# The first FFN's gate and up products as seven block products per slab, with the activations in six parts

## The chip, the cores and the metric

The kernel runs on one NeuronCore of a Trainium2 chip, as one launch. The metric is the device time of that core in microseconds (us). The profile splits the core into TensorE (PE, with its weight loads as PEld), VectorE (DVE), ScalarE (ACT), GpSimd (POOL) and SyncE (SP), which issues the DMAs. The engines run their own instruction streams in order and meet only at semaphores.

## The reference

A two-layer transformer trunk on 512 latent and 256 context tokens, 1024 wide: layer 0 mixes with gated linear attention, layer 1 with windowed attention, and each layer ends in a SwiGLU FFN with 2816 hidden units. The change touches the FFN of layer 0, which runs on all 768 tokens:

```python
def swiglu(h, w_in, w_out):
    g, u = jnp.split(h @ w_in, 2, axis=-1)
    return (jax.nn.silu(g) * u) @ w_out

x = x + g2 * swiglu(rmsnorm(x, norm_ffn[i]) * (1.0 + sc2) + sh2, ffn_w_in[i], ffn_w_out[i])
ctx = ctx + cg2 * swiglu(rmsnorm(ctx, norm_ffn[i]) * (1.0 + csc2) + csh2, ffn_w_in[i], ffn_w_out[i])
```

The gains sc2, sh2, g2 come from another product, SiLU(c) with `w_ada` (1024 x 6144 for each layer), of which the kernel computes 256 columns at a time: a "unit". Everything is float32.

## The kernel before

**Slabs.** All weights pass through in slabs of 256 columns. A slab is loaded (1 MB where it has 1024 rows), ACT copies it to `w_hi` in TensorE's rounded float32 format (L1260), DVE subtracts to get the rest `w_lo` (L1749, over the raw slab), and TensorE adds up three products for each pair of blocks: `w_hi x_hi`, `w_hi x_lo`, `w_lo x_hi` (L609). There are two slab buffers, and two sets of three PSUM banks. SP loads slab n once slab n-2 is done (`slab_done`), TensorE starts slab n when its `w_lo` is there (`wlo_ok`) and its banks are free (`out_free`).

**The first FFN** (`ffn(0, F0)`) has 34 slabs. 22 are gate/up slabs: 128 gate and 128 up columns, 8 k-chunks, all 768 tokens, first the 512 latent ones, then the 256 of the context. That is 48 matmuls of 512 columns and 48 of 256. After such a slab ACT applies SiLU to the gate (L1547), DVE multiplies by the up part (L2228), ACT rounds (L1550) and DVE subtracts (L2234), which gives one 128-row chunk of activations `a_hi`, `a_lo`. The chunks come in three parts of 8, 8 and 6 (`PARTS`), since the buffer holds 8. After each part come four down slabs, which multiply the part by 256 columns of `w_out`, and DVE adds the result to `xT` (`residual`, L1863, four instructions). A down slab has as many k-chunks as the part has chunks.

**Units.** 28 of these 34 slabs also carry a unit: SP loads 1 MB of `w_ada` into the one buffer `ada_w`, after the unit before has been used (`ada_done`); DVE multiplies and adds it up over 16 instructions (`unit_acc`, L1848 and L1852), TensorE sums over partitions (`unit_sum`, four small matmuls, in the trace eight records with their halves), and DVE stores the result (`store_sum`, L1830 to L1837).

**Order on DVE.** In a gate/up slab: `unit_acc` of the slab, the split of the next slab, `store_sum`, the multiply, the subtract. In a down slab: `unit_acc`, the split of the next, `store_sum`, the residual. DVE and ACT run in the order written; nothing schedules them.

**The head.** Before the FFN, DVE and ACT make `h_hi` and `h_lo` chunk by chunk (`normal`, L1803 and L1812; `modulate`, L1310), while TensorE already works on the raw rows of the first slab.

Of the kernel before, what the change touches and what calls it, by code (L numbers as in the profile page):

```python
# [24 lines left out]
F32 = mybir.dt.float32  # L25
# [7 lines left out]
P = 128  # L33
# [20 lines left out]
KV0 = F0 + FFN_SLABS  # L54
# [13 lines left out]
def trunk(nc, x, c, ctx_in, c_ctx, w_ada, b_ada, norm_mix, norm_ffn, gla_w_in, gla_w_gate_up, gla_b_gate_up,  # L68
# [26 lines left out]
    w_hi = [at(f"w_hi{s}", W + 2 * s * SLAB, [P, DC, 256], F32R) for s in range(2)]  # L95
    w_raw = [at(f"w_raw{s}", W + (2 * s + 1) * SLAB, [P, DC, 256]) for s in range(2)]
    w_lo = [at(f"w_lo{s}", W + (2 * s + 1) * SLAB, [P, DC, 256], F32R) for s in range(2)]
# [5 lines left out]
    a_lo = at("a_lo", A + DC * ROW, [P, DC, T], F32R)  # L103
    gla_q = at("gla_q", A, [P, GH, 4, T])
# [12 lines left out]
    ssq = at("ssq", TM + 6 * ROW, [P, T])  # L117
    ada_pre.append(ada_w)
# [130 lines left out]

    gw_ok, gwh_ok, gwl_ok, gl_done, gl_ok = sem("gw_ok"), sem("gwh_ok"), sem("gwl_ok"), sem("gl_done"), sem("gl_ok")  # L250
# [139 lines left out]
    def _(sp):  # L390
        def load_slab(n, i, pieces, kc=8):
# [4 lines left out]
            elif Q0 < n < SO0:  # L396
# [3 lines left out]
                sp.wait_ge(whi_ok, n - 1)  # L400
# [206 lines left out]
    def _(pe):  # L607
# [3 lines left out]
        def slab(n, i, rhs, segs, kc=8, before={}, k_wait=None, turns=None, by_chunk=False, sums=None, between=None,  # L611
# [6 lines left out]
            pe.wait_ge(wlo_ok, n + 1 + 2 * i)  # L618
# [9 lines left out]
            for z, (chunks, sgs) in enumerate(passes):  # L628
                for k in range(kc):
# [176 lines left out]
        def first_slab(n, e, segs, turn=None):  # L806
# [6 lines left out]
            pe.wait_ge(wlo_ok, n + 1)  # L813
# [89 lines left out]
        def fill(h, k, ch):  # L903
# [3 lines left out]
            if k == 0 and ch == 0:  # L907
                pe.wait_ge(wlo_ok, n + 1)
# [1591 lines left out]
```

## Time and profile before

| what | value |
|---|---|
| time, median of 3 runs | 1621.3 us (1621.28 to 1621.32) |
| span of the profiled execution | 1618.6 us; the runs are 2.7 us above it |
| PE busy | 1582.3 us, 98% of the span |
| PEld busy | 1345.5 us, 83% |
| DVE busy | 920.9 us, 57% |
| ACT busy | 575.2 us, 36% |
| chain that ended last | PE 86%, DVE 5%, ACT 5% |
| granted TensorE clock | full, but for the first slice (0.8) |
| DMA | 156.2 MB, mean 97 GB/s |

The busy share of PE counts modelled ends that overlap, so the pace of TensorE is read from the distance between the starts of its matmuls. The chain names the work that each later piece waited for. The profiled execution's own time beside its span isn't recorded; the runs above stand for it.

### The profile page before, as it was taken

To read this page: it belongs to the slowest core of one execution; us is meant where nothing else is said; L and a number is where in the kernel's file an instruction comes from. 1 tells how busy PE (TensorE), PEld (TensorE's weight loads), DVE (VectorE), ACT (ScalarE), POOL (GpSimd) and SP (SyncE) were. 2 spreads that over 40 slices of the span, in tenths; PEclk is the share of its full clock that TensorE was granted. 3 is DMA by queue.
4 is the path that set the end of the run, shared out by engine and by line. 5 is a ranking of instruction groups with operands and counts; after the bars stand their busy time and mean duration, and the time that the engine had idled before them with its cause. 6 is when DMAs were issued, how large, how long until landed. Compare 5 with 4: busy or idle time off the path is not lost.

```text
span 1618.6 us, 23967 instructions
## 1 busy us (share of the span) xinstructions
PE 1582.3 (98%) x9424; PEld 1345.5 (83%) x9424; DVE 920.9 (57%) x1592; ACT 575.2 (36%) x829; POOL 100.3 (6%) x95
## 2 busy tenths in 40 slices
PE   7999999999999999999999999989999999999998
PEld 5789988888888888888888888877778888888886
DVE  5665536544576667556666555888856533333334
ACT  5225457542342111122102124567744431222222
POOL 0000000000000000000000000046630000000003
PEclk8999999999999999999999999999999999999999
DMA  9442300013234334433343413320002323332332
GB/s 334 117 132 71 113 27 27 27 53 105 79 105 129 119 122 123 128 119 116 130 125 109 130 59 111 109 74 1 2 27 79 104 85 97 104 99 83 104 91 91
DMA packets 197438, 156.20 MB, mean 97 GB/s; under 512 B 6754, under 2 KB 194318, under 8 KB 197358
## 3 DMA queue, kind: packets, MB, share of 16 engines
q1 hardware_dynamic: 197358, 155.10, 31.5%
q8 instruction: 54, 0.88, 0.2%
q14 instruction: 26, 0.21, 0.1%
HBM read 149.84 MB, written 2.10 MB: 94 GB/s over the span
## 4 chain that ended last, share of the span: by engine, by line
PE 86%; DVE 5%; ACT 5%; issue 1%; DMA 1%; SPq 1%; DVEq 0%; ACTq 0%
PE ps L609 84%; PE ps L1145 1%; ACT pr L1703 1%; DVE w_lo L1749 1%; DMA ada_pre<-in_w_ada 1%; DVE scaled L1803 1%; DVE h_lo L1812 1%; ACT w_hi L1260 1%; PE ps L1150 1%; SPq L407 0%; DVE row_max L2394 0%; DVE q_st L2339 0%; ACT h_hi L1310 0%; DMA w_raw<-in_ffn_w_out 0%; ACT r_act L1460 0%
## 5 line engine op out<-in xcount | busy, mean ns | idle before, releaser
L609 PE MATMUL ps<-h_hi,w_hi 128*128 128x512 f32 (+1 forms) x1392 | 499.9, 359 | 1.4 <-DVE w_lo L1749 1.4
L609 PE MATMUL ps<-h_lo,w_hi 128*128 128x512 f32 (+1 forms) x1392 | 490.6, 352 | 0.0
L609 PE MATMUL ps<-h_hi,w_lo 128*128 128x512 f32 (+1 forms) x1392 | 490.4, 352 | 0.0
L1749 DVE TENSOR_TENSOR w_lo<-w_raw,w_hi 128x2048 fp32r<-128x2048 f32 (+1 forms) x88 | 197.1, 2240 | 201.9 <-ACT w_hi L1260 201.9
L609 PEld LDWEIGHTS ps<-h_hi,w_hi 128*128 128x128 f32 x1392 | 263.7, 189 | 47.0 <-issue 10.7
L1260 ACT ACTIVATE w_hi<-w_raw 128x2048 fp32r<-128x2048 f32 (+1 forms) x88 | 165.2, 1877 | 374.4 <-DMA w_raw<-in_ffn_w_in 200.0
L609 PEld LDWEIGHTS ps<-h_hi,w_lo 128*128 128x128 f32 x1392 | 263.6, 189 | 36.3
L609 PEld LDWEIGHTS ps<-h_lo,w_hi 128*128 128x128 f32 x1392 | 264.0, 190 | 35.7
L609 PE MATMUL ps<-a_hi,w_hi 128*128 128x512 f32 (+1 forms) x528 | 187.9, 356 | 0.1
L609 PE MATMUL ps<-a_lo,w_hi 128*128 128x512 f32 (+1 forms) x528 | 186.9, 354 | 0.0
L609 PE MATMUL ps<-a_hi,w_lo 128*128 128x512 f32 (+1 forms) x528 | 186.7, 354 | 0.0
L1852 DVE SCALAR_TENSOR_TENSOR u_acc<-ada_w,c_pre,u_acc 128x256 f32<-128x256 f32 x448 | 180.0, 477 | 0.0
L597 POOL TENSOR_SCALAR pr<-pr,rden 128x384 f32<-128x384 f32 x64 | 82.6, 1298 | 819.8 <-DVE rden L2406 819.5
L1547 ACT ACTIVATE tmp<-ps 128x512 f32<-128x512 f32 (+1 forms) x63 | 30.8, 524 | 259.4 <-PE ps L609 259.4
L609 PEld LDWEIGHTS ps<-a_hi,w_hi 128*128 128x128 f32 x528 | 99.8, 189 | 15.9 <-issue 1.6
L609 PEld LDWEIGHTS ps<-a_hi,w_lo 128*128 128x128 f32 x528 | 99.8, 189 | 13.9
L609 PEld LDWEIGHTS ps<-a_lo,w_hi 128*128 128x128 f32 x528 | 99.8, 189 | 13.6
L1830 DVE TENSOR_TENSOR u_acc<-ps,every 128x128 f32<-128x128 f32 x32 | 9.4, 293 | 140.1 <-PE ps L609 140.1
L1863 DVE SCALAR_TENSOR_TENSOR xT<-ps,mods,xT 128x256 f32<-128x256 f32 (+3 forms) x94 | 56.3, 654 | 56.8 <-PE ps L609 55.2
L609 PE MATMUL ps<-go,w_hi 128*128 128x256 f32 (+1 forms) x256 | 65.0, 345 | 0.3 <-ACT r_act L1460 0.3
L2228 DVE TENSOR_TENSOR tmp<-tmp,ps 128x512 f32<-128x512 f32 (+1 forms) x63 | 35.8, 596 | 48.7 <-ACT tmp L1547 48.7
L2234 DVE TENSOR_TENSOR a_lo<-tmp,a_hi 128x768 f32 (+3 forms) x42 | 34.7, 825 | 43.1 <-ACT a_hi L1550 43.1
(264 smaller groups left out, 1986.8 us busy)
## 6 DMA issues: line engine op xcount, KB each, us to landing
w_raw<-in_ffn_w_in SPq DMA_DIRECT2D x88, 512.0 KB, 4.9
ada_w<-in_w_ada SPq DMA_DIRECT2D x41, 1024.0 KB, 5.2
w_raw<-in_ffn_w_out SPq DMA_DIRECT2D x32, 512.0 KB, 4.4
w_raw<-in_gla_w_in SPq DMA_DIRECT2D x24, 512.0 KB, 4.9
ada_pre<-in_w_ada SPq DMA_DIRECT2D x7, 1024.0 KB, 11.6
w_raw<-in_ffn_w_out SPq DMA_DIRECT2D x16, 384.0 KB, 3.6
w_raw<-in_gla_w_o SPq DMA_DIRECT2D x8, 512.0 KB, 6.8
w_raw<-in_swa_w_o SPq DMA_DIRECT2D x8, 512.0 KB, 4.7
```

What stands on the lines that cost most here:

```text
L597: pool.tensor_scalar(pr[i % 4][:, 0:384], pr[i % 4][:, 0:384], rden[:, i % 4:i % 4 + 1], None, ALU.mult)\
L609: return pe.matmul(o, w, r, start=start, stop=stop, skip_group_check=skip)
L1145: last = pe.transpose(bank(4 + r, t * P, P), pr[i % 4][:, t * P:(t + 1) * P], ident[:, :])
L1150: last = pe.transpose(bank(6, (r * (nb - 3) + t - 3) * P, P), pr[i % 4][:, t * P:(t + 1) * P], ident[:, :])
L1260: act.activation(w_hi[s][:, 0:kc, :], raw_of(n)[:, 0:kc, :], ACT.Copy).then_inc(whi_ok, 1)
L1547: last = act.activation(tmp[s][:, sg[0]:sg[1]], seg(3 * s, 0, sg), ACT.Silu)
L1703: act.activation(pr[i % 4][:, 0:nk + 1], ps[:, sb:sb + nk + 1], ACT.Exp, bias=neg_max[:, i % 4:i % 4 + 1], scale=HD ** -0.5, accum_out=den ...
L1749: dve.tensor_tensor(w_lo[s][:, 0:kc, :], raw_of(n)[:, 0:kc, :], w_hi[s][:, 0:kc, :].bitcast(F32), ALU.subtract).then_inc(wlo_ok, 1)
L1852: last = dve.scalar_tensor_tensor(acc[:, m, :], ada_w[:, k, :], c_pre[:, k, m:m + 1], acc[:, m, :], ALU.mult, ALU.add)
L1863: last = dve.scalar_tensor_tensor(xs, seg(slab_banks(n), ch, sg), mods[:, bass.ds(gate + d0 + ch, 1), int(sg == CTX)], xs, ALU.mult, ALU.add)
L2228: last = dve.tensor_tensor(tmp[2 + s][:, sg[0]:sg[1]], tmp[s][:, sg[0]:sg[1]], seg(3 * s, 1, sg), ALU.mult)
L2234: dve.tensor_tensor(lo, tmp[2 + s][:, a:T], hi.bitcast(F32), ALU.subtract).then_inc(a_ok, 1)
```

## The change

The first three gate/up slabs stay as they were. In each of the other 19, the 256 x 1024 weight block times the 1024 x 768 token block is seen as 2 x 2 times 2 x 2 blocks: gate and up rows by two halves of k, two halves of k by two halves of 384 tokens. Strassen's scheme in Winograd's form computes it with seven block products in place of eight. Each product has 4 k-chunks, three matmuls each, of 384 columns: 84 matmuls a slab.

- Weights: four sums of blocks (`form_sum`, 512 elements a partition) on DVE, seven forms rounded by ACT (`form_high`) and seven subtractions by DVE (`form_low`), in place of one copy and one subtraction of 2048 elements.
- Tokens: once, after h is made. ACT writes the full h as well (`h_full`), DVE makes four sums and four low parts, ACT four high parts, 1536 elements each.
- Results: ACT copies partial sums out of PSUM (`part_sum`, four of 384 elements), DVE adds (`gate_sum_one`, `up_sum_one`, `up_sum_two`, `gate_sum_two`), then SiLU in two halves, the multiply and the split of the activations.
- There is one buffer for each form, so a form of the next slab waits for the product that used it in this one.
- Parts of 4, 4, 4, 3, 3, 4 chunks in place of 8, 8, 6: the first FFN has 24 down slabs in place of 12, with 3 or 4 k-chunks each. The token sums need the room.
- Units stand in a table: all four down slabs of the first three parts, two of the next two, and the last one to three gate/up slabs of a part. There are 28 as before.
- The first FFN is written out, not looped.

```diff
+PARTS0 = [(0, 4), (4, 4), (8, 4), (12, 3), (15, 3), (18, 4)]
...
+        if part_ == 0 and j_ == 3 or 0 < part_ < 5 and j_ >= fc_ - 2 or part_ == 5 and j_ > 0:
+            UNIT_AT[n_ + j_] = 12 + len(UNIT_AT)
...
+        def product(n, j):
+            q, s = SEVEN[n], n % 2
+            if j == 0:
+                pe.wait_ge(out_free[s], n // 2)
+            if q == 0 and j in (1, 3, 4, 5):
+                pe.wait_ge(sl_ok, (1, 3, 4, 5).index(j) + 1)
+            if j in (3, 4, 5):
+                pe.wait_ge(sn_ok, 4 * q + j - 2)
+            if j == 6:
+                pe.wait_ge(g_ok, q + 1)
+            pe.wait_ge(fl_ok, 7 * q + j + 1)
...
+        def part_sum(n, i):
+            act.wait_ge(pd_ok, 6 * q + (1, 2, 4, 6)[i])
+            if i == 1:
+                act.wait_ge(a_ok, IN0[n] - 1)
+            act.activation(dst, bank(b0 + int(i == 1), 0, HT), ACT.Copy).then_inc(sn_ok, 1)
...
+                if after:
+                    form_sum(n + 1, 0)
+                    form_low(n + 1, 0)
+                gate_sum_one(n)
+                if last_a is not None:
+                    store_sum(last_a)
+                if after:
+                    form_sum(n + 1, 1)
+                    form_sum(n + 1, 2)
+                    form_low(n + 1, 1)
+                    form_low(n + 1, 2)
+                    up_sum_one(n)
+                    if a_ is not None:
+                        unit_acc(a_)
+                    form_low(n + 1, 3)
+                    form_sum(n + 1, 3)
+                    up_sum_two(n)
+                    form_low(n + 1, 4)
+                    form_low(n + 1, 5)
...
+                gate_sum_two(n)
+                if after:
+                    form_low(n + 1, 6)
+                times_gate(n)
+                low0(n)
...
+                if last_a is not None:
+                    store_sum(last_a)
+                if a_ is not None:
+                    unit_acc(a_)
+                if e < 3:
+                    split(n + 1, 0, fc)
+                if part < 5:
+                    residual(n, 0, BOTH, 40, 2 * e, None)
```

**DVE in a gate/up slab.** Before, the end of one slab in the loop: the split of the next (2048 elements), `store_sum`, the multiply and the subtract.

```order
L1830 TENSOR_TENSOR u_acc_131<-ps,every_133 128x128 [waits or_ok,turned]
L1833 ISA
L1834 TENSOR_REDUCE den<-u_acc_131 128x4 [waits up_ok]
L1835 REGISTER_ALU
L1837 ISA [waits up_ok]
L1837 TENSOR_TENSOR mods<-den,vec 128x4
L2226 REGISTER_ALU
L2228 TENSOR_TENSOR tmp_83<-tmp_81,ps 128x256 [waits sg_ok]
L2228 TENSOR_TENSOR tmp_83<-tmp_81,ps 128x512
L2234 ISA [waits ah_ok]
L2234 TENSOR_TENSOR a_lo<-tmp_83,a_hi 128x768
```

After, the second half of a slab without a unit. `t_lo` and `w_lo_62` are low parts of the next slab's forms, `t_sum` a sum of its blocks, `tmp` the gate and up values.

```order
L2562 TENSOR_TENSOR t_lo_107<-t_sum_102,form_hi_65 128x512 [waits fh_ok]
L2562 TENSOR_TENSOR w_lo_62<-w_raw_60,form_hi_66 128x4x128 [waits fh_ok]
L2583 TENSOR_TENSOR tmp_97<-ps,tmp_97 128x384 [waits sn_ok,pd_ok]
L2562 TENSOR_TENSOR t_lo_108<-t_sum_103,form_hi_67 128x512 [waits fh_ok]
L2557 TENSOR_TENSOR t_sum_104<-w_raw_60 128x512 [waits pd_ok]
L2588 TENSOR_TENSOR tmp_97<-tmp_95,tmp_97 128x384 [waits sn_ok]
L2562 TENSOR_TENSOR w_lo_62<-w_raw_60,form_hi_68 128x4x128 [waits fh_ok]
L2562 TENSOR_TENSOR t_lo_109<-t_sum_104,form_hi_69 128x512 [waits fh_ok]
L2593 TENSOR_TENSOR tmp_95<-ps,tmp_95 128x384 [waits slab_done]
L2562 TENSOR_TENSOR t_lo_111<-t_sum_106,form_hi_70 128x512 [waits fh_ok]
L2598 TENSOR_TENSOR tmp_97<-tmp_95,tmp_97 128x768 [waits sg_ok]
L2538 TENSOR_TENSOR a_lo<-tmp_97,a_hi 128x768 [waits ah_ok]
```

Where one split and two multiplies stood, DVE now does form work for the next slab between the sums that free this slab's banks.

**DVE in a down slab.** Before: the residual of the slab behind its wait, then the unit of the next slab.

```order
L1863 ISA [waits slab_done]
L1863 ISA
L1863 SCALAR_TENSOR_TENSOR xT<-ps,mods,xT 128x256
L1863 ISA
L1863 SCALAR_TENSOR_TENSOR xT<-ps,mods,xT 128x512
L1863 ISA x2
L1863 SCALAR_TENSOR_TENSOR xT<-ps,mods,xT 128x256
L1863 ISA
L1863 SCALAR_TENSOR_TENSOR xT<-ps,mods,xT 128x512
L1842 REGISTER_ALU
L1848 TENSOR_SCALAR u_acc_131<-ada_w,c_pre 128x256 [waits in_unit]
L1848 TENSOR_SCALAR u_acc_131<-ada_w,c_pre 128x256
```

After: the split (1024 elements) for the next slab, the residual of this one, `store_sum`, the next unit.

```order
L2005 TENSOR_TENSOR w_lo_63<-w_raw_61,out_hi_w_72 128x1024 [waits whi_ok]
L2121 SCALAR_TENSOR_TENSOR xT<-ps,mods,xT 128x256 [waits slab_done]
L2121 SCALAR_TENSOR_TENSOR xT<-ps,mods,xT 128x512
L2121 SCALAR_TENSOR_TENSOR xT<-ps,mods,xT 128x256
L2121 SCALAR_TENSOR_TENSOR xT<-ps,mods,xT 128x512
L2088 TENSOR_TENSOR u_acc_155<-ps,every_157 128x128 [waits or_ok,turned]
L2092 TENSOR_REDUCE den<-u_acc_155 128x4 [waits up_ok]
L2095 TENSOR_TENSOR mods<-den,vec 128x4 [waits up_ok]
L2106 TENSOR_SCALAR u_acc_155<-ada_w,c_pre 128x256 [waits in_unit]
```

The four kinds of work are the same, the split is half as long, and there are twice as many slabs over which they come.

**PE at the third product.** Before, a gate/up slab has waits at its first matmul only (this is the end of one and the start of a down slab).

```order
L609 MATMUL ps<-h_hi,w_hi_59 128x256
L609 MATMUL ps<-h_lo,w_hi_59 128x256
L609 MATMUL ps<-h_hi,w_lo_63 128x256
L1053 REGISTER_ALU
L1053 COMPARE_AND_BRANCH
L1068 UNCONDITIONAL_BRANCH
L1068 ISA
L625 REGISTER_ALU [waits wlo_ok]
L609 MATMUL ps<-a_hi,w_hi_58 128x512 [waits a_ok,out_free0]
L609 MATMUL ps<-a_lo,w_hi_58 128x512
```

After, between the third and the fourth product of a slab:

```order
L677 MATMUL ps<-h_hi,form_hi_66 128x384
L677 MATMUL ps<-h_lo,form_hi_66 128x384
L677 MATMUL ps<-h_hi,w_lo_62 128x384
L677 MATMUL ps<-h_sums_hi,form_hi_67 128x384 [waits fl_ok,sn_ok]
L677 MATMUL ps<-h_sums_lo,form_hi_67 128x384
L677 MATMUL ps<-h_sums_hi,t_lo_108 128x384
L677 MATMUL ps<-h_sums_hi,form_hi_67 128x384
```

The fourth product waits for its form's low part and for ACT's copy of the first partial sum (`sn_ok`).

## Rows read from the trace of the kernel before

**Rows 1.** Busy time by engine: stretch, PE, PEld, DVE, ACT, POOL, PEclk, DMA.

```profile
466.00:980.00 514.00, 513.33 (x3086) 447.09 (x3087) 329.09 (x682) 101.95 (x107) 0.00 (x0) 1.00 0.38 118
```

**Rows 2.** The chain of waits about the first FFN: start, us, what.

```profile
462.40 1.81 ACT w_hi L1260
...
464.24 2.30 DVE w_lo L1749
...
466.67 533.36 PE ps L609 x3207
```

**Rows 3.** Timeline of PE in a gate/up slab pair: start, us, matmul.

```profile
632.02 0.39 PE L609 MATMUL ps<-a_lo,w_hi 128*128 128x512 f32 x1
632.25 0.39 PE L609 MATMUL ps<-a_hi,w_lo 128*128 128x512 f32 x1
632.47 0.28 PE L609 MATMUL ps<-a_hi,w_hi 128*128 128x256 f32 x1
632.59 0.28 PE L609 MATMUL ps<-a_lo,w_hi 128*128 128x256 f32 x1
```

**Rows 4.** Timeline of PE in the attention scores: 384 columns.

```profile
1109.76 0.85 PE L609 MATMUL ps<-k_st,q_st 128*128 128x384 f32 x4
1110.45 0.28 PE L609 MATMUL ps<-m_both,ident_b 128*128 128x256 bf16 x1
```

**Rows 5.** Timeline of DVE over one gate/up slab that carries a unit.

```profile
655.29 0.29 DVE L1830 TENSOR_TENSOR u_acc<-ps,every 128x128 f32<-128x128 f32 x1 [5.61 <-PE ps L609]
...
656.09 0.16 DVE L1837 TENSOR_TENSOR mods<-den,vec 128x4 f32 x1 [0.18 <-DVE den L1834]
657.07 1.02 DVE L2228 TENSOR_TENSOR tmp<-tmp,ps 128x256 f32<-128x256 f32 x2 [0.82 <-ACT tmp L1547]
659.24 0.96 DVE L2234 TENSOR_TENSOR a_lo<-tmp,a_hi 128x768 f32 x1 [1.15 <-ACT a_hi L1550]
660.11 0.61 DVE L1848 TENSOR_SCALAR u_acc<-ada_w,c_pre 128x256 f32<-128x256 f32 x2
660.64 5.62 DVE L1852 SCALAR_TENSOR_TENSOR u_acc<-ada_w,c_pre,u_acc 128x256 f32<-128x256 f32 x14
666.18 2.28 DVE L1749 TENSOR_TENSOR w_lo<-w_raw,w_hi 128x2048 fp32r<-128x2048 f32 x1
```

**Rows 6.** Timeline of DVE in a down slab: residual, then the unit.

```profile
622.06 2.19 DVE L1863 SCALAR_TENSOR_TENSOR xT<-ps,mods,xT 128x256 f32 x4 [0.21 <-issue]
624.17 0.60 DVE L1848 TENSOR_SCALAR u_acc<-ada_w,c_pre 128x256 f32<-128x256 f32 x2
```

**Rows 7.** Groups of DVE instructions by form: busy us, mean ns, idle before.

```profile
L1852 DVE SCALAR_TENSOR_TENSOR u_acc<-ada_w,c_pre,u_acc 128x256 f32<-128x256 f32 x448 | 180.0, 477 | 0.0
...
L2228 DVE TENSOR_TENSOR tmp<-tmp,ps 128x512 f32<-128x512 f32 x42 | 28.7, 684 | 31.9 <-ACT tmp L1547 31.9
...
L2228 DVE TENSOR_TENSOR tmp<-tmp,ps 128x256 f32<-128x256 f32 x21 | 8.8, 421 | 16.8 <-ACT tmp L1547 16.8
...
L2385 DVE TENSOR_TENSOR w_lo<-w_raw,w_hi 128x512 fp32r<-128x512 f32 x8 | 5.4, 672 | 0.0
```

**Rows 8.** Groups of ACT instructions by form.

```profile
L1547 ACT ACTIVATE tmp<-ps 128x512 f32<-128x512 f32 x42 | 25.0, 595 | 65.2 <-PE ps L609 65.2
...
L1663 ACT ACTIVATE w_hi<-w_raw 128x512 fp32r<-128x512 f32 x8 | 5.1, 632 | 0.0
```

**Rows 9.** DMA issues from 600 to 800 us: count, KB, us to landing.

```profile
ada_w<-in_w_ada SPq DMA_DIRECT2D x11, 1024.0 KB, 5.2
```

**Rows 10.** Timeline of ACT while the h vectors are made.

```profile
449.58 1.36 ACT L1310 ACTIVATE h_hi<-scaled,mods 128x512 fp32r<-128x512 f32 x2 [0.84 <-DVE scaled L1803]
```

**Rows 11.** Busy time by engine early in the kernel, columns as in rows 1.

```profile
20.00:31.00 11.00, 8.61 (x83) 4.89 (x81) 6.17 (x11) 6.24 (x10) 0.00 (x0) 0.71 1.10 350
```

**Rows 12.** Timeline of PE just after that stretch.

```profile
32.11 0.63 PE L609 MATMUL ps<-h_hi,w_lo 128*128 128x512 f32 x1
32.53 0.63 PE L609 MATMUL ps<-h_hi,w_hi 128*128 128x512 f32 x1
```

More of the change, by code:

```diff
@@ L1069, in ffn @@
                     for e in range(2):
[L1070 removed]
+                        slab(n + e, i, a_in, segs, kc=fc, k_wait=ready)
                 if l == 1 and after:
@@ L1074, in ffn, with ready @@
                 n += 4
-        ffn(0, F0, BOTH, 2)
+        def product(n, j):
[9 more added lines that the diff above has]
+            pe.wait_ge(fl_ok, 7 * q + j + 1)
+            o = bank(slab_banks(n) + (0, 1, 2, 0, 1, 0, 2)[j], 0, HT)
+            low = form_from(n, j, w_lo, t_lo)
+            x_hi, x_lo = token_form(j)
+            for k in range(4):
+                for i, (w, x) in enumerate(((form_hi[j], x_hi), (form_hi[j], x_lo), (low, x_hi))):
+                    last = mm(o, w[:, k, :], x[:, k, :], start=(k == 0 and i == 0 and j in (0, 1, 2, 6)),
+                              stop=(k == 3 and i == 2), skip=True)
+            last.then_inc(pd_ok if j < 6 else slab_done, 1)
+        first_slab(F0, 0, BOTH, turn=U1 - 1)
+        slab(F0 + 1, 0, h_in, BOTH, k_wait=h_wait(1, 2), joint=True)
+        slab(F0 + 2, 0, h_in, BOTH)
+        for n in range(F0 + 3, KV0):
+            if n in SEVEN:
+                for j in range(7):
+                    product(n, j)
+                    if j == 1 and n - 1 in UNIT_AT:
+                        unit_sum(UNIT_AT[n - 1])
+            else:
+                part, e, fc = OUT0[n]
+                done = PARTS0[part][0] + fc
+                def ready(k, done=done, fc=fc):
+                    if k in (0, fc - 1):
+                        pe.wait_ge(a_ok, done - (k == 0))
+                slab(n, 0, a4_in, BOTH, kc=fc, k_wait=ready,
+                     before={(0, 1): lambda: unit_sum(UNIT_AT[n - 1])} if n - 1 in UNIT_AT else {})
         first_slab(KV0, KV_EDGE, BOTH)
@@ new lines, in _ @@
+        modulate(1, 0, BOTH, sh, 0, 2)
+        bias_row(0)
+        modulate(1, 0, BOTH, sh, 2, 6)
+        act.wait_ge(bz_ok, 1)
+        act.wait_ge(zg_ok, 1)
+        for sg in BOTH:
+            last = act.activation(tmp[0][:, sg[0]:sg[1]], tmp[0][:, sg[0]:sg[1]], ACT.Silu,
+                                  bias=bz[:, 0, int(sg == CTX):int(sg == CTX) + 1])
+        last.then_inc(sg_ok, 1)
+        modulate(1, 0, BOTH, sh, 6, 8)
+        split(n + 2)
+        act.wait_ge(zp_ok, 1)
+        act.activation(a4_hi[:, 0, :], tmp[2][:, :], ACT.Copy).then_inc(ah_ok, 1)
@@ new lines, in _ @@
+        n, sh = F0, 24
+        inverse(5)
+        normal(1, 0, BOTH, sh, 0, 1)
+        split(n + 1)
+        normal(1, 0, BOTH, sh, 1, 6)
+        dve.wait_ge(slab_done, n + 1)
+        dve.tensor_copy(bz[:, :, :], bank(7, 0, 4).rearrange("p (c m) -> p c m", m=2)).then_inc(bz_ok, 1)
+        for sg in BOTH:
+            last = dve.tensor_tensor(tmp[0][:, sg[0]:sg[1]], seg(0, 0, sg), rb[:, sg[0]:sg[1]], ALU.mult)
+        last.then_inc(zg_ok, 1)
+        for sg in BOTH:
+            last = dve.tensor_tensor(tmp[2][:, sg[0]:sg[1]], seg(0, 1, sg), rb[:, sg[0]:sg[1]], ALU.mult)
@@ new lines, in _ @@
+        last.then_inc(out_free[0], 1)
+        normal(1, 0, BOTH, sh, 6, 8)
+        split(n + 2)
+        dve.wait_ge(out_free[0], n // 2 + 1)
+        dve.wait_ge(sg_ok, 1)
+        for sg in BOTH:
+            c_ = int(sg == CTX)
+            last = dve.scalar_tensor_tensor(tmp[2][:, sg[0]:sg[1]], tmp[2][:, sg[0]:sg[1]], bz[:, 1, c_:c_ + 1],
+                                            tmp[0][:, sg[0]:sg[1]], ALU.add, ALU.mult)
+        last.then_inc(zp_ok, 1)
+        low0(n)
+        dve.wait_ge(hf_ok, DC)
```

362 lines of the change are left out of this document (316 added, 46 removed).

## The prediction

> **What bounds the kernel now.** I read the page first: TensorE is busy for 98% of the span, the chain that ended last is 86% TensorE. Then the windows over the stretch in question, from 466 us (third gate/up slab) to 980 us: TensorE is busy 513 of 514 us at the full clock, VectorE 329 us, ScalarE 102 us, DMA at 0.38 [rows 1]. Then the chain: from 466.67 us on it is one unbroken piece of TensorE [rows 2]. So removed matmul time comes back in full as long as VectorE keeps up. The reader is to see the other side too: VectorE is the second engine, at 64%, and the change gives it work and takes none of its large items away.
>
> **TensorE, what goes.** Matmuls start 0.23 us apart at 512 columns (632.02, 632.25, 632.47) and 0.12 at 256 [rows 3]. So a gate/up slab before is 48 x 0.2265 + 48 x 0.12 = 16.64 us. At 384 columns four take 0.69 us, 0.173 each [rows 4]; a slab of seven products is 84 x 0.1733 = 14.56 us. Nineteen slabs save 19 x 2.08 = 39.5 us. Down slabs keep their matmuls in sum: 8.32 us with four chunks (24 of each width), 6.24 with three. A unit's sums cost TensorE 0.56 us, as before.
>
> **VectorE, what comes.** Durations: 512 elements take 0.672 us [rows 7], but successors start 0.08 us before the end: 14 unit instructions of 0.477 fill 5.62 us, 0.40 each [rows 5, 7]. I take 0.60 for 512 elements. 384 elements from PSUM lie between 0.421 and 0.684 [rows 7]: 0.55, in a row 0.47. 768 elements: 0.96, in a row 0.87 [rows 5]. A unit: 660.11 to 666.18 = 6.07. Storing it: 655.29 to 656.25 = 0.96, with its waits 1.05. Residual: 622.06 to 624.17 = 2.11 [rows 6]. Split: 2.28 for 2048 elements [rows 5], 1.1 for 1024.
> A seven-product slab then has 11 form instructions (6.6), four sums (1.9), multiply and subtract (1.75): 10.25 us, where before split, multiply and subtract made 4.2. Two round trips over ScalarE stand in its order: 1.15 us before the subtract, as now [rows 5], and about as much before the multiply (half a SiLU, 0.46, and the last form, 0.63 by [rows 8], between `gate_sum_two` and `form_low` 6). That is 12.5 us, within 14.56. With a unit it is 18.6, 4.0 too long.
>
> At the whole of a part of four with six units VectorE has 4 x 10.25 + 4 x 1.1 + 4 x 2.11 + 6 x 7.05 = 96 us of work; TensorE has 58.2 + 33.3 + 6 x 0.56 = 94.9. Before, TensorE had 103.2 for the same and VectorE some 67. The two engines are now level, and each wait of one for the other is lost. Where the waits come:
>
> - Slab after a unit slab: its fourth product needs ScalarE's copy of the first partial sum, and that stands in ScalarE's queue behind the rounding of the late activations. TensorE waits the 4.0 us. The first down slab then waits for the last chunk: after `slab_done` come sum 0.55, SiLU 0.46, multiply 0.96, rounding 0.85, subtract 0.96 and hand-overs, 4.2 us, and that slab's last chunk comes after 4.1; with a store and unit in front of it, 1.4 us.
> - First to second down slab: 4.2, store 1.05, unit 6.07, split 1.1, hand-over 0.2: 12.7 against 8.9, so 3.8.
> - Second to third, third to fourth: `ada_w` is one buffer. The load is issued when a unit ends and lands 5.2 us later [rows 9], with 0.2 for the issue, then 6.07: 11.5 from unit to unit, against 8.9. VectorE's own work (10.4) is nearly as long. 2.6 each.
> - Fourth to next part: unit, one sum and one form in place of the split, then the residual (2.11) between forms 1 and 2: 2.9.
>
> Parts 1 and 2: 94.9 + 4.0 + 1.4 + 3.8 + 5.2 + 2.9 = 112.2 against 103.2, +9.0 each, **+18.0**. Part 0 (one new slab): -2.1 + 3.8 + 5.2 + 2.9 = **+9.8**. Parts 3 and 4 (three chunks, units in two gate/up and two down slabs): TensorE 43.7 + 25.0 + 2.2 = 70.9; waits 4.0, 1.0, then 12.4 against 6.8 (5.6), and 2.4 after the third down slab, with 0.4: 84.3 against 77.1, +7.2 each, **+14.4**. Part 5 (three unit slabs in a row, none in its down slabs): -8.3 + 4.2 + 5.0 + 1.5 = **+2.4**.
>
> **The head.** ScalarE has 0.84 us free per chunk of h [rows 10] and gets 1.05 more (`h_full`, two copies). Chunks come about 0.5 us later each, six times, and the last two add 1.4 before ScalarE reaches the copy of the third slab, which starts TensorE's unbroken run [rows 2]: 4.4 us. After it VectorE has, beside the old work, four token sums of 1.76 (1536 elements by the 2048 row) and two low parts: the first product of the first new slab is ready 18.5 us after that start, where TensorE comes after 16.6: 1.9. Two more low parts, a unit and a split then stand ahead of the first down slab, 4.8 late. **+11.2**; bounds 3 (all but the first 4.4 hidden) and 16.
>
> Sum: 18.0 + 9.8 + 14.4 + 2.4 + 11.2 = +55.8 us. The profiled execution's span is 1618.6 and the runs' median 1621.3; 2.7 lie around the span, untouched. 1621.3 + 55.8 = **1677 us**, a span of 1674.
>
> Not in the sum: six-part residuals on the last part's ScalarE and VectorE chain (squares, raw rows) fit 8.3 us with little to spare, 0 to 3 us. SP gets 24 loads more of half the size, on a queue that is idle, 0.
>
> **A rule against the trace.** The 14 unit instructions start 0.40 us apart though each lasts 0.477 [rows 5, 7], so they overlap. The Trainium skill, "VectorE: DVE Perf Modes", section "The DRAIN you can't avoid", says the next operation doesn't start before the pipe has emptied. The trace disagrees by those 0.08 us an instruction.
> As a mechanism of its own, VectorE starting each instruction only at the end of the one before, it would give 19 x 11 x 0.07 + 28 x 16 x 0.077 = 49 us more, 1726; I give it 0.01.
>
> **Rivals.**
> 1. The waits pack. VectorE works through without a hole, since the sum of its work, 96 us, is what a part takes, under 103.2. The place is the down slabs: if `ada_w` came earlier than 5.2 us and ScalarE's trips fell beside form work, parts 1 and 2 would gain 7 each, 3 and 4 6 each, part 5 8, part 0 2, less 8 for the head, 28 in all: 1593. It decides once the holes of a part stay under 7 us. Against it: both of the trips are there in the present trace, with nothing to put in between, and they alone are 2.3 us a slab.
> 2. VectorE hides all, as the diff's interleaving seems to aim at: 1621.3 - 39.5 = 1582. Against it stands the 18.6 us of a unit slab.
> 3. It costs more. The unit's load now meets the slab's, issued 1.3 us behind it; at the 16 unit loads next to down slabs up to 1.7 us more each (half a slab's share of 5.2 us), 27 us. And the clock: where TensorE stood idle for a fifth of the time the granted clock was 0.71 [rows 11], and matmuls of 512 columns started 0.42 us apart [rows 12] in place of 0.23, the lower of its levels, 1.2 GHz. There are now some 25 holes of 2.5 to 5.6 us. A block product (12 x 0.173 = 2.1 us) at half pace costs 2.1 more; behind holes in down slabs such a loss is mostly hidden by the unit, in gate/up slabs not. 0 to 25 us. Together up to 1729; I take 1707 for this case.
> The Trainium skill, "TensorE: Matmul & The Clock Gate", section "HAM oscillation — how this bites in real kernels", says that a wait repeated in each tile throttles the engine again each time; that is this rival's second half, and the present trace has too few holes in this stretch to say.
> 4. The change doesn't do what it says: half the slabs wait for token sums or forms and no order results. Nothing in the waits points to it.
>
> **Chances.** Forecast (slower, 1652 to 1695) 0.69. No overlap on VectorE 0.01. Rival 3 0.17. Rival 1 0.07, rival 2 0.02. Small waits that about cancel, within 0.2% of 1621 (what a measurement of this kernel can tell): 0.02, and a small loss up to 1652, 0.02. So faster 0.09, same 0.02, slower 0.89. The range for eight in ten, 1645 to 1708: at its low end the head costs 3 and the parts' 84 us of waits are three tenths less, at its high end half of rival 3 comes in, and 3 to 5 on the last part's chain.
>
> **What would show it.** In the profile after: PE busy in the first FFN falls by about 40 us while the stretch gets longer; VectorE over 85% busy there. Matmuls of 384 columns 0.173 apart. The down slabs with units start 11.5 us apart, the first of each part 12.7 after its start. In gate/up slabs, the hole is before the fourth product, released by a ScalarE copy from PSUM. `ada_w` lands 5.2 us after its issue, or 7 (rival 3). PEclk under 1.00 in those slices would be rival 3's other half. The prediction is wrong if units run in less than 6 us, or if VectorE shows under 75%.

## The result, and the profile after

The changed kernel takes 1681.8 us (median of four runs, 1680.6 to 1687.1) against 1621.3: a ratio of 1.038, interval 1.036 to 1.040. It is slower by 60.5 us; the forecast was 55.8, 1677. The profiled execution is the longest of the four, span 1685.4, and its +66.8 is what the lines below add up to; the spans of the other three runs were 1678.9 to 1680.7, 4.7 to 6.5 us shorter.

The page, busy time by engine, and the chain of waits:

```profile
span 1685.4 us, 23337 instructions
PE 1584.0 (94%) x9196; PEld 1363.8 (81%) x9196; DVE 1083.0 (64%) x1907; ACT 665.2 (39%) x1051; POOL 100.1 (6%) x95
PE 68%; DVE 18%; ACT 6%; DMA 4%; issue 3%; SPq 1%; DVEq 0%; ACTq 0%
```

Over the whole span VectorE is busy 64% of the time, 57% before. The stretch has to be read by itself; there it was 64% before [rows 1]. These are windows of the profile after (columns as in [rows 1]): the part of four chunks from 551 to 664 us, a part of three, and the whole to 1064, where the FFN ends; the unbroken piece of TensorE at full clock of [rows 1, 2] is gone.

```profile
551.00:664.00 113.00, 102.42 (x571) 93.54 (x572) 95.83 (x202) 34.70 (x60) 0.00 (x0) 0.92 0.37 112
777.00:862.00 85.00, 72.64 (x403) 66.25 (x402) 71.31 (x149) 25.56 (x45) 0.00 (x0) 0.92 0.35 105
466.00:1064.00 598.00, 533.68 (x2979) 482.56 (x2977) 502.62 (x1009) 190.79 (x321) 0.00 (x0) 0.93 0.35 105
```

VectorE works 95.8 us in the first of these windows, near the 96 of the forecast for a part, and 84% of the whole stretch. TensorE's waits from 466 to 1060 us, sorted by what ended them (us in total, times, longest):

```profile
PE ps L677 <- DVE w_lo L2005: 35.7, 14, 3.9
PE ps L677 <- ACT tmp L1752: 21.3, 6, 3.7
PE ps L677 <- DVE w_lo L2562: 4.6, 3, 2.4
PE ps L677 <- DVE a_lo L2538: 1.5, 2, 0.7
```

They come to 63 us. One sign that the forecast named didn't come: TensorE's busy time in the first FFN was to fall by about 40 us. It is 533.7 us (last window above) against 531.3 before (466 to 998 us), though 39.5 us of matmuls are gone: many of those that are left take longer, as the last rows of this section show.

The two large rows are the two kinds that the forecast named: the split of a down slab's weights behind a unit, and ScalarE's copy of the first partial sum. The second kind, in ScalarE's timeline at a slab after a unit slab:

```profile
606.93 0.84 ACT L1764 ACTIVATE a_hi<-tmp 128x768 fp32r<-128x768 f32 x1 [1.63 <-DVE tmp L2598]
607.68 0.85 ACT L1752 ACTIVATE tmp<-ps 128x384 f32<-128x384 f32 x2
```

The copy (L1752) is ready to go long before, but stands behind the rounding of the activations (L1764), and that waits for VectorE's multiply (L2598), late by the unit. TensorE meets it before the fourth product:

```profile
608.21 0.69 PE L677 MATMUL ps<-h_sums_hi,form_hi 128*128 128x384 f32 x1 [3.52 <-ACT tmp L1752]
```

The first kind, in the chain of waits over two down slabs (start, us, what):

```profile
635.98 5.55 DVE u_acc L2110 x14
...
641.55 5.24 DMA ada_w<-in_w_ada
...
646.81 0.62 DVE u_acc L2106 x2
647.42 4.83 DVE u_acc L2110 x13
...
652.99 5.22 DMA ada_w<-in_w_ada
```

Unit, load, unit, load: 11.44 us from one load to the next (641.55, 652.99), with nothing else in it. The load has its 5.24 us, as before [rows 9]. And TensorE, where such a hole ends, starts at half pace, 0.43 us apart at 512 columns in place of the 0.23 of [rows 3]:

```profile
631.29 0.80 PE L677 MATMUL ps<-a_hi,out_hi_w 128*128 128x512 f32 x1 [3.08 <-DVE w_lo L2005]
631.88 0.63 PE L677 MATMUL ps<-a_lo,out_hi_w 128*128 128x512 f32 x1
632.31 0.63 PE L677 MATMUL ps<-a_hi,w_lo 128*128 128x512 f32 x1
```

That is the lower of the clock's two levels, 1.2 GHz, as in [rows 12]; the granted clock is 0.92 to 0.93 over the parts, and was 1.00. Of the 18 holes of 2 us and more between 466 and 1064 us, 16 are followed by matmuls at that pace, even the shorter ones (551.77, after 2.42 us; 654.15, after 2.24); the holes of under 1 us leave next to none. This agrees with the Trainium skill, "TensorE: Matmul & The Clock Gate", section "HAM oscillation — how this bites in real kernels", that waits which come again in each tile throttle the engine again each time.

### The profile page after: what moved, and what is told of

The parts are those of the page before. It is cut to its first block, busy times and chain, and to the rows that moved or that the text cites. A ratio compares the mean times of both kernels' runs of the same rounds, so it can differ in the third digit from the quotient of the medians.

```text
span 1685.4 us, 23337 instructions
## 1 busy us (share of the span) xinstructions
PE 1584.0 (94%) x9196; PEld 1363.8 (81%) x9196; DVE 1083.0 (64%) x1907; ACT 665.2 (39%) x1051; POOL 100.1 (6%) x95
## 4 chain that ended last, share of the span: by engine, by line
PE 68%; DVE 18%; ACT 6%; DMA 4%; issue 3%; SPq 1%; DVEq 0%; ACTq 0%
PE ps L677 66%; DVE u_acc L2110 7%; DMA ada_w<-in_w_ada 2%; DVE w_lo L2005 1%; PE ps L1257 1%; DVE t_lo L2562 1%; DMA w_raw<-in_ffn_w_in 1%; ACT w_hi L1375 1%; ACT pr L1959 1%; DVE t_sum L2557 1%; DVE u_acc L2106 1%; DMA ada_pre<-in_w_ada 1%; DVE w_lo L2562 1%; DVE scaled L2061 1%; DVE tmp L2598 1%
## 5 line engine op out<-in xcount | busy, mean ns | idle before, releaser
L677 PE MATMUL ps<-h_hi,w_lo 128*128 128x512 f32 (+2 forms) x936 | 338.0, 361 | 0.0
L677 PE MATMUL ps<-h_hi,w_hi 128*128 128x512 f32 (+1 forms) x784 | 293.7, 375 | 4.2 <-DVE w_lo L2005 4.0
L677 PE MATMUL ps<-h_lo,w_hi 128*128 128x512 f32 (+1 forms) x784 | 286.4, 365 | 0.0
L677 PEld LDWEIGHTS ps<-h_hi,w_hi 128*128 128x128 f32 x784 | 148.5, 189 | 34.5 <-issue 6.2
L677 PEld LDWEIGHTS ps<-h_lo,w_hi 128*128 128x128 f32 x784 | 148.7, 190 | 24.0
L677 PE MATMUL ps<-a_hi,out_hi_w 128*128 128x512 f32 (+1 forms) x352 | 128.6, 365 | 35.2 <-DVE w_lo L2005 33.7
L677 PE MATMUL ps<-a_lo,out_hi_w 128*128 128x512 f32 (+1 forms) x352 | 124.4, 353 | 0.0
L677 PE MATMUL ps<-h_hi,form_hi 128*128 128x384 f32 x304 | 103.7, 341 | 5.0 <-DVE w_lo L2562 4.6
L677 PE MATMUL ps<-h_sums_lo,form_hi 128*128 128x384 f32 x304 | 106.7, 351 | 0.0
L677 PE MATMUL ps<-h_lo,form_hi 128*128 128x384 f32 x304 | 104.4, 343 | 0.0
L677 PE MATMUL ps<-h_sums_hi,form_hi 128*128 128x384 f32 x152 | 55.1, 363 | 21.3 <-ACT tmp L1752 21.3
## 6 DMA issues: line engine op xcount, KB each, us to landing
ada_pre<-in_w_ada SPq DMA_DIRECT2D x7, 1024.0 KB, 11.5
```

What stands on the lines that cost most here:

```text
L677: return pe.matmul(o, w, r, start=start, stop=stop, skip_group_check=skip)
```

## The experiments

Kernels of one group ran on one chip, with the kernel before beside them: 1622.0 us in the first group, 1621.6 in the second, 1621.4 in the third.

### 1. Less of a unit's work

```diff
-            for k in range(DC):
+            for k in range(1 if a >= 12 else DC):
...
+                    dve.wait_ge(mod_ok, last_a + 2)
```

`unit_acc` then has 2 instructions in place of 16. The second line makes VectorE, in a down slab, wait for its own store of the last unit.

> The changed kernel, with the 28 units of the first FFN computing one of their eight k-chunks on VectorE (2 instructions in place of 16; the other seven are left out). Loads, TensorE sums and stores stay. Theory (VectorE's unit work on top of the form work makes the holes): a unit costs 0.6 us in place of 6.1, VectorE falls to some 60% of a part, the holes of 2.5 to 4 us go and with them the half-pace stretches; left are about 1 us at each part's start of down slabs and the head's 4 us. 1590 to 1600 us. Rival A (the form work alone, or ScalarE's round trips, makes the holes): holes in gate/up slabs stay, over 1630. Rival B (twice as many down slabs cost by themselves): the holes between down slabs stay, over 1630.

Measured: 1593.0 us, ratio 0.982 (0.981 to 0.984), inside the expectation. The same shortening of the units on the kernel before (without that wait), as a control:

> The kernel before with the same units shortened in the same way (seven of eight k-chunks left out). VectorE was 64% busy there and never waited for: every theory expects 1621 us within 1.

Measured: 1621.6, ratio 0.9997 (0.9987 to 1.0007). So the units cost nothing before, and 89 us after. Without them the change does bring a gain, 29 us. A window of that run (its parts of four start at 537.94, 633.06 and 728.46 us):

```profile
551.00:664.00 113.00, 113.00 (x680) 105.89 (x679) 77.84 (x140) 43.47 (x76) 0.00 (x0) 1.00 0.43 131
```

TensorE is never idle, and VectorE works 69% of the window. The matmul arithmetic of the forecast stands: 94.9 us were worked out for TensorE in such a part, and the starts are 95.1 and 95.4 apart.

### 2. Six parts alone

The parts, the table of units and all else of the change, but ordinary slabs: no token sums, no forms.

```diff
-        if f_ + j_ >= 3:
-            SEVEN[n_ + j_] = f_ + j_ - 3
...
-                for j in range(7):
-                    product(n, j)
...
+                slab(n, 0, h_in, BOTH,
+                     before={(0, 1): lambda: unit_sum(UNIT_AT[n - 1])} if n - 1 in UNIT_AT else {})
```

> The changed kernel with ordinary gate/up slabs in place of the seven products (no forms, no token sums), but with its six parts, 24 down slabs and its table of units. Theory: the down slabs with units are bound by unit to unit, 5.2 for the load, 0.2 and 6.1, 11.5 us against TensorE's 8.9, whatever the gate/up slabs do: 12 us a part in parts 0 to 2, 8 in parts 3 and 4, so 1621 + 53 = 1674, and up to 10 more by half pace after the holes. No hole in gate/up slabs. Rival (the form work on VectorE is what costs): 1621 to 1630 us, since VectorE is back to 4.2 us a gate/up slab.

Measured: 1685.8, ratio 1.040 (1.039 to 1.042), at the top of what was expected (1674 and up to 10 more), and no faster than the whole change. TensorE does the full eight products here, and VectorE in a part of four works only 66.4 us of 113:

```profile
551.00:664.00 113.00, 106.64 (x620) 90.03 (x618) 66.42 (x145) 18.61 (x20) 0.00 (x0) 0.96 0.34 103
```

So a net loss of this size needs no form work at all. It takes short down slabs: TensorE passes one in 8.9 us and the chain of unit and load takes 11.5. The holes stand at the starts of the slabs that follow one another there, all behind the split: 2.89, 0.96 and 2.51 us at part 1's down slabs, and 2.32 at the first slab of the next part. Inside gate/up slabs there is none. The first of them:

```profile
630.14 0.50 PE L673 MATMUL ps<-a_hi,w_hi 128*128 128x512 f32 x1 [2.89 <-DVE w_lo L1958]
```

The whole change takes 39.5 us of matmuls away and adds the waits behind ScalarE's copy, 21.3 us, with some 14 us of half pace in the slabs where they stand (2 to 3 us in each of six). The two nearly cancel: 1681.8 against 1685.8, with intervals that overlap.

### 3. Both: six parts, short units

In the kernel of experiment 2:

```diff
-            for k in range(DC):
+            for k in range(1 if a >= 12 else DC):
```

> Six parts and the new unit table with ordinary gate and up slabs, as in the six-parts run, and each unit's sum cut from 16 VectorE instructions to 2 (one of eight k-chunks). Theory (the loss of six parts is units' work in short down slabs, nothing else of size; a seven-product slab is worth 2.08 us once VectorE keeps up): this kernel stands 39.5 us above the short-unit run of the seven products (1593), so 1628 to 1636. Rival (six parts cost of themselves, by 12 more down slabs with their splits and edges, and the seven products gain less than 2.08 each): then it is either over 1645 (six parts cost) or under 1620 (the products gain less).

Measured: 1640.9, ratio 1.011 (1.009 to 1.013), between the two expectations. With room on VectorE the seven products are worth 47.9 us (1640.9 - 1593.0), 8 more than their matmuls, and six parts cost 19 by themselves. The extra is at the first slab of each part, where an ordinary slab waits for the split of all its 2048 columns:

```profile
748.93 0.50 PE L673 MATMUL ps<-h_hi,w_hi 128*128 128x512 f32 x1 [1.42 <-DVE w_lo L1958]
...
831.29 0.50 PE L673 MATMUL ps<-h_hi,w_hi 128*128 128x512 f32 x1 [3.28 <-DVE w_lo L1958]
...
914.58 0.80 PE L673 MATMUL ps<-h_hi,w_hi 128*128 128x512 f32 x1 [3.19 <-DVE w_lo L1958]
```

A seven-product slab needs a quarter of that before its first product, and in experiment 1 waits 0 to 1 us there.

The four kernels with six parts also say how the costs meet. The units' VectorE work costs 45 us with ordinary slabs (1685.8 - 1640.9) and 89 us with seven products (1681.8 - 1593.0). So 45 us of the loss are units in short down slabs, 19 the six parts themselves, and 44 come only where units and form work share VectorE; they eat most of the 47.9 us that the seven products are worth without the units' work (45 + 19 + 44 - 47.9 is the 60 us of the result).

### 4. Half of a unit's work

```diff
-            for k in range(DC):
+            for k in range(4 if a >= 12 else DC):
```

> The changed kernel with 8 of a unit's 16 VectorE instructions (k-chunks 0 to 3 alone; the modulation values lack the rest): 3.1 us less for VectorE in each of 28 units, loads unchanged. Theory A (each wait is a chain that outlasts its slab by 2 to 4 us, so the first 3 us taken away remove nearly all of the waits): 1600 to 1618. Theory B (VectorE's sum over the stretch is what counts, so the gain goes with the work: 3.1 of the 5.4 us that were worth 89 us): 1628 to 1634.

Measured: 1600.7, ratio 0.987 (0.985 to 0.989). Half of the work gives 81 of the 89 us: theory A. The waits are hinges, not a share of the sum: a wait stands where a chain outlasts its slab, and is gone once it doesn't. With 3.1 us less, load and unit take 8.4 us, under the slab's 8.9, TensorE runs without a break through part 1's down slabs, where the change has three holes (first row, the chain from 600 to 640 us), and elsewhere stubs remain:

```profile
599.94 40.08 PE ps L677 x251
```

```profile
588.69 0.44 PE L677 MATMUL ps<-h_sums_hi,form_hi 128*128 128x384 f32 x1 [0.36 <-ACT tmp L1752]
...
934.67 0.45 PE L677 MATMUL ps<-h_sums_hi,form_hi 128*128 128x384 f32 x1 [1.25 <-ACT tmp L1752]
```

### 5. A shorter load

```diff
-            sp.dma_start(ada_w[:, :, :], w_ada[l][:, bass.ds((e + i) * 256, 256)].rearrange("(k p) n -> p k n", p=P))\
+            q = 2 if a >= 12 else DC
+            sp.dma_start(ada_w[:, 0:q, :], w_ada[l][0:q * P, bass.ds((e + i) * 256, 256)]
+                         .rearrange("(k p) n -> p k n", p=P))\
```

> The changed kernel, with the load of a unit's ada_w cut to 2 of its 8 k-chunks (256 KB of 1 MB) for the first FFN's 28 units; VectorE still runs all 16 instructions of each unit, over what then stands in the buffer (the modulation values of the later stages are wrong by that). Theory (the chain load, sum, load, sum sets the pace of adjacent down slabs with units, and a load lands in some 5.2 us of which part is transfer): the load lands 1 to 3 us earlier, adjacent down slabs with units come 10.0 to 10.9 us apart in place of 11.5, and about 10 such places give 5 to 15 us: 1667 to 1677. Rival 1 (the loads' traffic holds back weights and what waits for them): a gain of over 20 us, under 1660. Rival 2 (VectorE is busy in that time anyway, with splits and sums that were put off): no change, 1680 to 1684.

Measured: 1672.9, ratio 1.032 (1.030 to 1.034), 9 us less than the change: the theory's case. The DMA issues of this run from 600 to 800 us, and its chain over one down slab:

```profile
ada_w<-in_w_ada SPq DMA_DIRECT2D x12, 256.0 KB, 2.8
```

```profile
636.08 2.06 PE ps L679 x14
638.16 0.30 DVE u_acc L2090
638.49 0.30 DVE den L2094
638.81 0.17 DVE mods L2097
638.97 0.53 DVE u_acc L2108 x2
639.50 5.54 DVE u_acc L2112 x14
645.04 1.15 DVE w_lo L2007
646.23 2.05 PE ps L679 x14
```

The load is 2.5 us shorter and out of the chain, and the slabs come 10.15 us apart (636.08, 646.23) in place of 11.44. In its place stands a loop that the forecast did not have: VectorE's store of the last unit waits for TensorE's sum, which stands in the slab behind its first chunk (2.06 us of TensorE), the slab waits for the split, and the split stands behind the unit. A wait that ends 2.5 us earlier gave 1.3, since the next one stood close behind. That the loads' traffic held much up (the first half of rival 3) is not borne out. It does show in a down slab's own loads, 256 KB each: from 600 to 800 us they land in 5.6 us in the change and in 3.3 here. But the chain that ended last goes through the units' loads there, not through them, and 9 us is no more than this chain explains.

### 6. Units elsewhere

```diff
+UNIT_AT = {n_: 12 + i_ for i_, n_ in enumerate((19, 20, 21, 22, 23, 25, 27, 29, 30, 31, 33, 35, 36, 37, 38, 39, 40, 42,
+                                                43, 45, 47, 49, 50, 52, 53, 55, 56, 57))}
```

> The changed kernel with another table of units: no two adjacent gate and up slabs have one (slabs 25, 27, 33, 35, 40, 42, 47, 49 in place of 26, 27, 34, 35, 41, 42, 48, 49), the first down slab of part 1 has none, and slab 53 has one. Theory (VectorE is filled to over 80% through the whole stretch, so moving units moves waits): 1673 to 1682. Rival (the waits come from how the units are crowded, and a spread table lets most of the 39.5 us through): under 1660.

Measured: 1684.0, ratio 1.038 (1.036 to 1.039), 2 us above the expectation and as the change itself. TensorE's waits, same stretch as above: those behind down slabs' splits and behind the copy stay (35.1 and 21.5 us), and those behind the first form of a part grow from 4.6:

```profile
PE ps L679 <- DVE w_lo L2564: 9.1, 4, 3.3
```

Spreading the units does not help, and by one table alone I can't say that none would.

### 7. Holes filled with unused matmuls

Twelve matmuls of 384 columns (0.20 us each), whose result nothing reads, ahead of each place where TensorE waits.

```diff
+                    if j == 0 and n - 1 in OUT0 and n - 1 in UNIT_AT or j == 3 and n - 1 in UNIT_AT and n - 1 in SEVEN:
+                        fill(12)
...
+                if n - 1 in UNIT_AT:
+                    fill(12)
```

> The changed kernel with 12 matmuls of 384 columns (2.1 us, into a bank that nothing uses then) before each place where TensorE waited: the down slab or next part after a unit slab, the fourth product after a unit slab. They compute nothing that is used. In the changed kernel's trace 184 matmuls ran at half pace after holes, 41 us more than at full pace. Theory: in gate/up slabs and in down slabs without unit that loss is on the path, behind VectorE it is hidden: the clock goes back to near 1.00, half-pace matmuls nearly vanish, 1655 to 1670 us. Rival (VectorE alone sets the time, the half pace is hidden everywhere): 1680 us or, by the added matmuls, more.

Measured: 1673.8, ratio 1.032 (1.031 to 1.034): 8 us faster than the change, by work that is thrown away, but 4 us above the expected range. The granted clock is back at 1.00 in the parts:

```profile
551.00:664.00 113.00, 110.81 (x659) 102.54 (x660) 98.72 (x207) 36.62 (x64) 0.00 (x0) 1.00 0.40 119
```

and the first matmuls of a down slab start 0.23 apart:

```profile
628.30 0.39 PE L677 MATMUL ps<-a_lo,out_hi_w 128*128 128x512 f32 x1
628.53 0.39 PE L677 MATMUL ps<-a_hi,w_lo 128*128 128x512 f32 x1
```

So rival 3's second half is real. In the changed kernel the matmuls at half pace made up some 30 us of TensorE's time (27 to 37, by what is counted as late; the expectation had 41). Only 8 came back, for two reasons. Where TensorE would have waited for VectorE anyway, a faster pace only makes the wait longer. And the 8 us are net of the fill's own cost: it also stands in front of each later part's first down slab, where TensorE hadn't waited (614.65 to 616.73 us, for one), 2.1 us in five places. By this the clock was worth more than 8 us; how much more no run shows.

### 8. The weight sums on GpSimd

```diff
+            pool.tensor_tensor(t_sum[(0, 1, 3 + q % 2, 2)[i]][:, :, :], a, b, ALU.subtract).then_inc(ts_ok, 1)
...
+            dve.wait_ge(ts_ok, 4 * SEVEN[n] + (1, 2, 3, 3, 4, 4, 3)[j])
...
-                    form_sum(n + 1, 0)
```

The second line stands in `form_low`: `w_lo` is written over `w_raw`, which the sums read, so every low part now waits for GpSimd, also those that use no sum.

> The changed kernel, full computation, with the weight sums t_sum of 18 of the 19 seven-product slabs (72 subtractions of 128x512) made by GpSimd in place of VectorE; the first slab's four stay on VectorE. GpSimd has nothing else to do in this stretch; its nearest row (128x512 tensor_scalar, one input) is 1.75 us, VectorE's sum is 0.60 start to start. Theory A (the two engines work side by side): VectorE has 43 us less, of which the half-unit run says nearly all comes back, less 1 to 3 us at each of the four later part heads where a sum stands in the chain to a product: 1640 to 1655. Theory B (an engine waits while the other one's operation with two SBUF inputs holds the port, as the Trainium skill, SBUF, has it): VectorE gets 43 us and loses up to 72 x 1.75 = 126 us: 1700 to 1755, and VectorE's u_acc and t_lo instructions show longer times. Between them (1665 to 1690): they block each other for part of the time only, or the sums' latency eats the gain.

Measured: 1706.7, ratio 1.052 (1.050 to 1.054): 25 us slower than the change, at theory B's near end, but for the most part not by B's mechanism. GpSimd needs 1.5 to 1.6 us for each sum (first row, of the whole run, for two of the four kinds of sum; the others are of 551 to 1040 us):

```profile
L682 POOL TENSOR_TENSOR t_sum<-w_raw 128x512 f32<-128x512 f32 x36 | 58.8, 1634 | 605.3 <-DMA w_raw<-in_ffn_w_in 576.9 <-PE ps L703 28.4
L2589 DVE TENSOR_TENSOR w_lo<-w_raw,form_hi 128x512 fp32r<-128x512 f32 x54 | 40.4, 748 | 41.5 <-POOL t_sum L682 41.5
L2589 DVE TENSOR_TENSOR t_lo<-t_sum,form_hi 128x512 fp32r<-128x512 f32 x72 | 59.8, 836 | 30.3 <-ACT form_hi L1758 17.9 <-POOL t_sum L682 12.3
```

By the last column the larger half is idle time: VectorE stands still for 54 us for those sums, 41.5 and 12.3, more than the 43 us it was freed of. The rest is the two engines' meeting. In the next two rows GpSimd's sum runs from 581.95 to 583.70, and VectorE's addition of two SBUF tiles in that time takes 1.65 us, where its mean was 0.55:

```profile
581.95 1.75 POOL L682 TENSOR_TENSOR t_sum<-w_raw 128x512 f32<-128x512 f32 x1 [1.26 <-PE ps L703]
```

```profile
582.47 1.65 DVE L2615 TENSOR_TENSOR tmp<-tmp,tmp 128x384 f32<-128x384 f32 x1
```

It ends 0.4 us after GpSimd does. The Trainium skill, "SBUF — State Buffer", section "SBUF: two separate sides", gives the rule: a VectorE operation with two SBUF inputs and a GpSimd operation that reads SBUF exclude each other for a whole instruction. This row agrees. The price of the blocking by itself, from VectorE's longer means (`t_lo` 687 to 836 ns, x72), is about 11 us on that group and some 24 over all of VectorE's groups, much less than the bound of 126: GpSimd mostly ran while VectorE waited for it.

No full kernel here beats the one before. What one would need is known from experiment 4: 3 us less VectorE work per unit, without a new wait. I found no other engine to give it to at that price; GpSimd with the unit's multiplications was not tried, nor was a second buffer for `ada_w`. It would take the load out of the chain as experiment 5 did, which gave 9 us.

## Why the prediction came out right

The direction and the size were right, and the kinds of wait. The sum, though, had too much for waits and nothing for the clock, and part of its closeness is luck. Against the profiled execution, term by term:

| step | forecast, us | measured, us | from |
|---|---|---|---|
| head | +11.2 | +6.2 | below |
| part 0 | +9.8 | +9.4 | 504.77 to 551.77, 0.4 under |
| parts 1, 2 | 112.2 each | 114.0, 113.3 | starts 551.77, 665.75, 779.06 |
| parts 3, 4 | 84.3 each | 90.8, 88.8 | starts 779.06, 869.88, 958.69 |
| part 5 | +2.4 | +4.2 | 958.69 to 1064.49 |
| sum | +55.8 | +66.1 | spans differ by 66.8 |

**VectorE's load.** Right. The 96 us of a part (96.8 and 96.6 busy in parts 1 and 2), 0.60 us from form to form, and 6.07 for a unit (594.73 to 600.79) came out, and from one unit slab's first sum to the next's 17.8 us (590.93 to 608.68) where 18.6 was worked out:

```profile
600.79 0.69 DVE L2562 TENSOR_TENSOR t_lo<-t_sum,form_hi 128x512 fp32r<-128x512 f32 x1
601.40 0.69 DVE L2557 TENSOR_TENSOR t_sum<-w_raw 128x512 f32<-128x512 f32 x1
```

They overlap by 0.08 us, so the reading of a VectorE that doesn't overlap, 1726, falls. The section of the Trainium skill that the prediction names there ("VectorE: DVE Perf Modes", "The DRAIN you can't avoid") also says that an operation that isn't held starts earlier, so these rows don't stand against it.

**The waits in the slabs.** Right in kind, and each somewhat too long: 3.52 (up to 3.7) before the fourth product where 4.0 was worked out, 11.44 from unit to unit for 11.5, first to second down slab 12.2 (619.13 to 631.29) for 12.7, and no wait for the last chunk in parts 1 and 2 where 1.4 was counted. The forecast's waits of the parts come to 84 us, the holes in the trace from 504.77 us on (without that first one) to 60.

**The clock.** The step that failed is that the sum has no term for matmuls at half pace. The prediction named them, said that in gate/up slabs they are not hidden and in down slabs "mostly hidden" by the unit, and counted both only in rival 3. They came to some 30 us. Where a unit's chain sets the pace they stand in time that was counted as a wait: the down slab at 631.29 has 1.5 us of it and is 11.42 long all the same. Elsewhere they add up. In part 3, against the forecast slab by slab:

- The last gate/up slab, with the wait for ScalarE's copy, takes 21.65 us for 19.1.
- The first gate/up slab takes 15.27 for 14.56: a unit's sums, 0.56, had been left out.
- The first down slab takes 11.9 for 13.4.
- The two down slabs without a unit of their own take 8.44 for 6.8 and 9.63 for 7.2, and the one between them 9.38 for 8.6.

That is 6.5 us in all, and 4.5 in part 4. The first of the two without a unit, behind its hole:

```profile
842.42 0.80 PE L677 MATMUL ps<-a_hi,out_hi_w 128*128 128x512 f32 x1 [3.85 <-DVE w_lo L2005]
843.02 0.63 PE L677 MATMUL ps<-a_lo,out_hi_w 128*128 128x512 f32 x1
843.44 0.63 PE L677 MATMUL ps<-a_hi,w_lo 128*128 128x512 f32 x1
...
846.18 0.39 PE L677 MATMUL ps<-a_lo,out_hi_w 128*128 128x512 f32 x1
846.41 0.40 PE L677 MATMUL ps<-a_hi,w_lo 128*128 128x512 f32 x1
```

Experiment 7 bears it out: with the clock held up, parts 3 and 4 take 84.9 and 84.2 us (starts 773.36, 858.23, 942.47), the forecast's 84.3. Part 5 is the same story: holes of 3.52, 3.69 and 1.33 us, 8.5 where 10.7 was counted, and 4.0 us of half pace behind the first two.

**The head.** Too high by 5.0 us, and right in one place by chance. The third slab started 2.1 us later than before (468.77 against [rows 2]'s 466.67), not 4.4. Of that, 0.9 stood there before the first of the new copies (ScalarE's `w_hi` at 439.07 against 438.18), and 1.0 is the last chunk's copy in front of `w_hi`. The other copies fit into the pace of 2.2 us a chunk that VectorE's work on h sets (starts 452.39, 454.60; before, 447.37, 449.58). The first product came 18.4 us after that start, as forecast (18.5), but not by the wait that was worked out: its form was ready after 17.1 us, and TensorE came 1.8 us late since eight matmuls of the third slab ran at half pace behind the hole:

```profile
468.77 0.50 PE L677 MATMUL ps<-h_hi,w_hi 128*128 128x512 f32 x1 [2.01 <-DVE w_lo L2005]
...
470.64 0.63 PE L677 MATMUL ps<-h_lo,w_hi 128*128 128x512 f32 x1
471.07 0.63 PE L677 MATMUL ps<-h_hi,w_lo 128*128 128x512 f32 x1
```

The first down slab's hole was 2.25 us, not 4.8.

**The rivals.** Rival 1 and rival 2 needed load and unit to fit in 8.9 us; they do only with half of the unit's work (1600.7, near rival 1's 1593). Of rival 3's traffic little shows: `ada_w` lands in 5.24 us, and one load of a gate/up slab, in part 5, takes 7.86 us on the chain (992.07), where the next hole is 3.69 us in place of 3.52. Its clock is the term above. Rival 4 does not hold, since seven products gain 47.9 us once VectorE has room.

**Luck.** The parts were 15.3 us too low and the head 5.0 too high, and the profiled execution is 5.4 us above the median; so a sum that is 10.3 us short of the trace comes within 5 us of the measured 60.5.

What stays open is why the profiled execution is longer than the other runs; they have no trace.

## What to carry to other kernels

Before cutting a slab's work on the busiest engine, write down each loop that must fit into a slab (load into a single buffer, the work on it, the hand-back) and compare it with the shortest slab after the change: here cutting the FFN into six parts made slabs of 8.9 us around a loop of 11.5, and the six parts alone cost 64 us, 45 of them by the units in that loop, more than the 39.5 us of matmuls saved. Such costs are hinges: half of the work taken out of the loop brought nine tenths of the loss back, while moving the work about, or to an engine that shares a port and adds its latency to the chain, brought nothing or less. Where waits come in, put the slower clock behind them into the sum wherever TensorE is the one that is waited for. And test the schedule change without the arithmetic change first; here it alone was as slow as both together.

## What the runs showed of the hardware

- Matmuls nobody reads made a kernel 8 us faster: 12 of 384 columns ahead of each wait held the granted clock at 1.00 where it was 0.92 (551 to 664 us).
- Holes of 2 to 4 us were followed by matmuls at half pace in 16 of 18 cases, 0.43 us apart at 512 columns; they were back at 0.23 within the same slab (842.42 and after, above).
- A load of 256 KB landed in 2.8 us and one of 1 MB in 5.2: a quarter of the bytes took over half of the time.
- GpSimd's subtraction of two 128x512 float32 tiles took 1.5 to 1.6 us, VectorE's 0.69 and 0.60 from start to start; and one VectorE operation on two SBUF tiles took three times as long beside it (1.65 us for 0.55).
